# Two transformer blocks on one core: later modulation columns, finer norm pieces with unread products at the joints, bias sums on VectorE

## The reference

```python
def first_block(x, c, ...):
    mod = (silu(c) @ w_ada + b_ada)              # 6 x 1024: shift, scale, gate for mixer and FFN
    h = rms_norm(x, g_pre_mix) * (1 + sc_m) + sh_m
    y = hybrid_mixer(h, ...)                     # NSA group + DSA group, then w_out
    x = x + ga_m * rms_norm(y, g_post_mix)
    h = rms_norm(x, g_pre_ffn) * (1 + sc_f) + sh_f
    return x + ga_f * rms_norm(swiglu(h, w_gate_up, w_down), g_post_ffn)

def compress(k, pe, w1, b1, w2, b2):             # inside the NSA group, for keys and for values
    blocks = k[:, idx] + pe                      # 31 overlapping blocks of 32 tokens
    return gelu(flatten(blocks) @ w1 + b1) @ w2 + b2
```

## Time and profile before

| | before |
|---|---|
| median of 3 runs | 2392.31 us |
| the profiled execution | 2389.78 us, of which the span is 2387.7 us |
| mean granted TensorE clock | 0.974 of full |
| TensorE (matmul) busy | 2284.4 us, 96% |
| VectorE / ScalarE / GpSimd busy | 43% / 21% / 29% |
| DMA, mean busy share of 16 engines | 33%, 105 GB/s |

### The profile page before, as it was taken

One profiled execution on the slowest core, in us unless ns is written; L12 is line 12 of the kernel. 1 busy time (PEld: TensorE's weight loads), 2 busy tenths in 40 slices (PEclk: granted clock), 3 DMA queues, 4 the chain that ended last, 5 costly groups with the idle time before them and its releaser, 6 DMA issues. The chain is left out here.

```text
span 2387.7 us, 26637 instructions
## 1 busy us (share of the span) xinstructions
PE 2284.4 (96%) x10499; PEld 1766.8 (74%) x10499; DVE 1022.1 (43%) x1899; ACT 492.3 (21%) x1131; POOL 683.5 (29%) x549
## 2 busy tenths in 40 slices
PE   7999999899999999999999999997999899999998
PEld 3454667667757888888778888884556668888887
DVE  4556854454325752244554223542623422112354
ACT  3101332233344000010300011112133532000002
POOL 0000000000010655564155555520010104555642
PEclk9999889899999999999999999998999999999999
DMA  9533334453421454233335432331122122222230
GB/s 323 178 133 105 108 103 145 159 169 101 120 77 65 141 172 146 66 85 81 106 111 171 141 95 66 81 106 35 36 75 71 36 71 71 71 96 70 73 98 36
DMA packets 255287, 250.14 MB, mean 105 GB/s; under 512 B 19874, under 2 KB 207420, under 8 KB 255036
## 3 DMA queue, kind: packets, MB, share of 16 engines
q1 hardware_dynamic: 254728, 248.30, 33.0%
q10 hardware_dynamic: 436, 0.15, 0.0%
HBM read 243.19 MB, written 4.19 MB: 104 GB/s over the span
## 5 line engine op out<-in xcount | busy, mean ns | idle before, releaser
L1975 POOL TENSOR_TENSOR w_sums<-ring 128x512 f32<-128x512 f32 x66 | 90.3, 1368 | 514.0 <-POOLq L1306 330.3
L2001 POOL TENSOR_TENSOR hidden<-rstd,h_act 128x256 f32<-128x256 f32 x66 | 53.8, 816 | 401.4 <-DVE h_act L2177 401.4
L1860 PE MATMUL ps<-h_sums,w_sums 128*128 128x256 f32 x528 | 128.9, 384 | 6.0 <-DVE h_sums L2113 5.6
L814 PE MATMUL ps<-h_act,ring 128*128 128x512 f32 (+1 forms) x288 | 128.3, 599 | 5.2 <-PEq L333 4.4
L2177 DVE TENSOR_TENSOR h_act<-ps,rstd 128x256 f32<-128x256 f32 x78 | 33.0, 424 | 232.3 <-PE ps L1878 136.1
L1878 PE MATMUL ps<-h_sums,ring 128*128 128x256 f32 x528 | 125.8, 381 | 2.5 <-DVE rstd L2156 2.2
L1866 PE MATMUL ps<-h_act,ring 128*128 128x256 f32 x528 | 126.5, 383 | 0.0
L1872 PE MATMUL ps<-h_sums,w_sums 128*128 128x256 f32 x528 | 125.1, 380 | 1.0 <-DVE rstd L2149 1.0
L1826 PE MATMUL ps<-h_act,ring 128*128 128x256 f32 x528 | 125.2, 381 | 0.0
L1883 PE MATMUL ps<-h_act,w_sums 128*128 128x256 f32 x528 | 124.7, 379 | 0.0
L1834 PE MATMUL ps<-h_act,ring 128*128 128x256 f32 x528 | 124.5, 379 | 0.0
(11 more groups left out here) (463 smaller groups left out, 4461.8 us busy)
## 6 DMA issues: line engine op xcount, KB each, us to landing
ring<-in_ffn_w_in SPq DMA_DIRECT2D x66, 1024.0 KB, 7.7
ring<-in_w_ada SPq DMA_DIRECT2D x12, 2048.0 KB, 7.9
ring<-in_w_mod SPq DMA_DIRECT2D x12, 2048.0 KB, 8.0
ring<-in_w_gate_up SPq DMA_DIRECT2D x22, 1024.0 KB, 8.0
ring<-in_ffn_w_out SPq DMA_DIRECT2D x32, 704.0 KB, 6.2
ring<-in_w_in SPq DMA_DIRECT2D x6, 2048.0 KB, 8.1
ring<-in_ffn_w_out SPq DMA_DIRECT2D x8, 1408.0 KB, 7.0
ring<-in_w_down SPq DMA_DIRECT2D x16, 704.0 KB, 5.8
```

Of the source, the lines that this page charges most:

```text
L814: last = pe.matmul(K.ps[i % 3][0:rows, :], lhs(w, item, j, k), hl(k), start=(k == 0), stop=(k == KT - 1))
L1860: last = pe.matmul(pb, s2[:, k], F.t2[:, k], start=(k == 0), stop=(k == 3))
L1975: pool.tensor_tensor(s1, a21, a22, ALU.add).then_inc(S["wsum"].sem, 1)
L2001: pool.tensor_tensor(one[:, j], F.gate1[f % 2], F.got21[f % 2], ALU.mult)
```

## The change

Four parts, in one diff.

1. Selector: the bias sum `pe @ w1` is formed by VectorE, 32 instructions of 128x128, two interleaved sums, before `weigh(1)`; TensorE needs one product for each of the two parts. `prob_scores(0)` and `(1)` come before the latent keys and values, and these take two context products after each, instead of none between and 8 afterwards. The number of context products before `prob_turn(0)` is the same (48).
2. Attention: `modulation_columns` for ada 4+j moves from tile f = 9+2j to f = 10+2j (the last two to down tiles 1 and 3), with two buffers for the sums instead of one.
3. Joints: x is updated and squared in three pieces (4, 2, 2 tiles of 128 features) instead of two, multiplied by the root in three (2, 3, 3); ScalarE scales all of the first half before it takes the second root; TensorE runs 15 products of ones by ones, 128 columns, that nobody reads, after `x_sum(0)` in the joints after out1, the first and second FFN and out2, and 38 at the end of `stage_ffn_1_2`.
4. Second FFN call: GpSimd starts its first weight sums when x is updated (before: when the normed h is written) and its second when VectorE's first eight h sums are done; VectorE starts the modulation sums at odd units in call 1.

```diff
@@ selector @@
+    pesum = K.sem("lc_pesum")
-    free = (2, 5, 3, 4)
...
                     if m % 4 == 3:
                         context(1)
-                for m in range(16):
-                    last = pe.matmul(K.ps[3 + i][:, 64:65], w[:, i, m, :], K.p("cmp_pe", 16 * i + m, 1),
-                                     start=(m == 0), stop=(m == 15))
-                    if m % 4 == 3 and m < 15:
-                        context(1)
-                last.then_inc(hidm, 1)
-                context(1)
+                pe.wait_ge(pesum, 31 + i)
+                pe.matmul(K.ps[3 + i][:, 64:65], M.cstd[:, P * i:P * i + P], K.ones[:, 0:1], start=True,
+                          stop=True).then_inc(hidm, 1)
+                context(4)
...
             pe.wait_ge(rel, 24)
-            for j in range(4):
-                if j == 2:
-                    pe.wait_ge(cmk, 2)
-                pe.matmul(K.ps[free[j]][:, :], M.wuk[:, 2 * j:2 * j + 2, :], M.cT[:, :], start=True, stop=False)
-                pe.matmul(K.ps[free[j]][:, :], const(K, "esel", ROPE), M.kr[:, :], start=False,
-                          stop=True).then_inc(kvm, 1)
-            for t in range(QT):
-                pe.wait_ge(kvk, t + 1)
-                pe.matmul(K.ps[free[t]][:, :], M.cT[:, t * P:t * P + P], M.wuv[:, :, :].rearrange("p h d -> p (h d)"),
-                          start=True, stop=True).then_inc(kvm, 1)
-            context(8)
-            pe.wait_ge(kvk, 4 + QT)
+            pe.wait_ge(cmk, 2)
             prob_scores(0)
             prob_scores(1)
-            context(40)
+            for n in range(4 + QT):
+                if n >= 2:
+                    pe.wait_ge(kvk, n - 1)
+                dst = K.ps[n % 2][:, :]
+                if n < 4:
+                    pe.matmul(dst, M.wuk[:, 2 * n:2 * n + 2, :], M.cT[:, :], start=True, stop=False)
+                    last = pe.matmul(dst, const(K, "esel", ROPE), M.kr[:, :], start=False, stop=True)
+                else:
+                    t = n - 4
+                    last = pe.matmul(dst, M.cT[:, t * P:t * P + P], M.wuv[:, :, :].rearrange("p h d -> p (h d)"),
+                                     start=True, stop=True)
+                last.then_inc(kvm, 1)
+                context(2)
+            context(32)
+            pe.wait_ge(kvk, 4 + QT)
             prob_turn(0)
... (VectorE, after the four norm products and before weigh(1))
+            w = K.ring.take(dve, "cmp").rearrange("p (i m h) -> p i m h", i=2, m=16)
+            for m in range(16):
+                for i in range(2):
+                    part, at = M.cstd[:, P * i:P * i + P], K.p("cmp_pe", 16 * i + m, 1)
+                    if m:
+                        dve.wait_ge(pesum, 2 * m - 1 + i)
+                        ins = dve.scalar_tensor_tensor(part, w[:, i, m, :], at, part, ALU.mult, ALU.add)
+                    else:
+                        ins = dve.tensor_scalar(part, w[:, i, m, :], at, None, ALU.mult)
+                    ins.then_inc(pesum, 1)
@@ attention @@
-    late_sums = lambda m, v: K.rstd[:, 0, :]
+    late_sums = lambda m, v: K.rstd[:, m % 2, :]
...
-            columns = {CTX_SCORER + 2 * j + 1: (("ada", 4 + j), late_sums) for j in range(7)}
+            columns = {CTX_SCORER + 2 * j + 2: (("ada", 4 + j), late_sums) for j in range(6)}
+            more = {1: (("ada", 10), late_sums), 3: (("ada", 11), late_sums)}
...
-                    context_down(K, X, pe, d, (("ada", 11), late_sums) if d == 1 else None) for d in range(KT)))
+                    context_down(K, X, pe, d, more.get(d)) for d in range(KT)))
...
-            steps = itertools.chain.from_iterable(modulation_steps(K, dve, ("ada", 4 + j), late_sums, 1)
+            steps = itertools.chain.from_iterable(modulation_steps(K, dve, ("ada", 4 + j), late_sums, 2)
@@ tails @@
+NEW_PIECES = ((0, 4), (4, 6), (6, KT))
+NORMED_PIECES = ((0, 2), (2, 5), (5, KT))
...
-    for b in range(2):
-        y = T.y(4 * b, 4 * b + 4, HALF * t, HALF * t + HALF)
-        S["turned"].wait(dve, 2 * t + b + 1)
-        dve.tensor_tensor(x_part(K, t, b), x_part(K, t, b), y, ALU.add).then_inc(S["x_new"].sem, 1)
+    for k0, k1 in NEW_PIECES:
+        y = T.y(k0, k1, HALF * t, HALF * t + HALF)
+        S["turned"].wait(dve, 2 * t + (1 if k1 <= 4 else 2))
+        dve.tensor_tensor(x_part(K, t, k0, k1), x_part(K, t, k0, k1), y, ALU.add).then_inc(S["x_new"].sem, 1)
...
+def idle_products(K, pe, bank, n):
+
+    for _ in range(n):
+        pe.matmul(K.ps[bank][:, 0:P], K.ones[:, :], K.ones[:, :], start=True, stop=True)
... (tail_scalar)
     h_scaled(K, T, act, 0, range(0, 4))
+    h_scaled(K, T, act, 0, range(4, KT))
     x_root(K, T, act, 1)
-    h_scaled(K, T, act, 0, range(4, KT))
... (end of out_tensor; the same with bank 2 at the end of fast_tail_tensor)
     x_sum(K, O.T, pe, 0, 1)
+    idle_products(K, pe, 5, 15)
... (stage_ffn_1_2, after the last fast_tail_tensor)
                 x_sum(K, F1.T, pe, 1, 1)
+                idle_products(K, pe, 2, 38)
@@ fast_gpsimd, fast_vector @@
     if call == 1:
-        F.prev.s["normed"].wait(pool, 4)
+        F.prev.s["x_new"].wait(pool, 6)
     up_weight_sums(0)
+    if call == 1:
+        S["hsum"].wait(pool, 8)
     up_weight_sums(1)
...
-            if u // 2 < len(F.late) and u % 2 == 0:
+            if u // 2 < len(F.late) and u % 2 == F.call:
                 steps = modulation_steps(K, dve, ("mod", F.late[u // 2]), late, 2)
```

More of the change, by code:

```diff
@@ L1504, in __init__ @@
         self.s = {n: Tally(K.tail[n], K.tail_base[n]) for n in TAIL_SEMS}
-        counts = dict(squared=len(pieces), scaled=len(pieces), added=len(self.adds), y_sum=2, y_root=2, turned=4, x_new=4)
+        counts = dict(squared=len(pieces), scaled=len(pieces), added=len(self.adds), y_sum=2, y_root=2, turned=4, x_new=6)
         if scale is not None:
-            counts.update(x_sq=4, x_sum=2, x_root=2, normed=4, h=2 * KT)
+            counts.update(x_sq=6, x_sum=2, x_root=2, normed=6, h=2 * KT)
         for n, count in counts.items():
@@ L1578, in x_update @@
         dve.tensor_tensor(y, y, r, ALU.mult).then_inc(S["turned"].sem, 1)
[L1579 to L1582 removed]
+    for k0, k1 in NEW_PIECES:
+        y = T.y(k0, k1, HALF * t, HALF * t + HALF)
+        S["turned"].wait(dve, 2 * t + (1 if k1 <= 4 else 2))
+        dve.tensor_tensor(x_part(K, t, k0, k1), x_part(K, t, k0, k1), y, ALU.add).then_inc(S["x_new"].sem, 1)
 def x_square(K, T, act, t):
[L1587 to L1589 removed]
+    for i, (k0, k1) in enumerate(NEW_PIECES):
+        T.s["x_new"].wait(act, 3 * t + i + 1)
+        act.activation(T.squares[t][:, k0:k1, :], x_part(K, t, k0, k1), ACT.Square).then_inc(T.s["x_sq"].sem, 1)
 def x_sum(K, T, pe, t, b):
[L1594 to L1596 removed]
+    for i in ((0,), (1, 2))[b]:
+        T.s["x_sq"].wait(pe, 3 * t + i + 1)
+        for k in range(*NEW_PIECES[i]):
+            last = pe.matmul(K.ps[6 + t][:, 0:HALF], K.ones[:, :], T.squares[t][:, k, :], start=(k == 0),
+                             stop=(k == KT - 1))
     if b:
@@ L1609, in x_normed @@
 def x_normed(K, T, dve, t):
-    r = K.tmp[:, 1, HALF * t:HALF * t + HALF].unsqueeze(1).broadcast_to([P, 4, HALF])
     T.s["x_root"].wait(dve, t + 1)
-    for b in range(2):
-        dve.tensor_tensor(h_part(K, t, b), x_part(K, t, b), r, ALU.mult).then_inc(T.s["normed"].sem, 1)
+    for k0, k1 in NORMED_PIECES:
+        r = K.tmp[:, 1, HALF * t:HALF * t + HALF].unsqueeze(1).broadcast_to([P, k1 - k0, HALF])
+        dve.tensor_tensor(h_part(K, t, k0, k1), x_part(K, t, k0, k1), r, ALU.mult).then_inc(T.s["normed"].sem, 1)
 def h_scaled(K, T, act, t, ks):
     for k in ks:
-        T.s["normed"].wait(act, 2 * t + k // 4 + 1)
+        T.s["normed"].wait(act, 3 * t + sum(k >= a for a, _ in NORMED_PIECES))
         h = K.h[:, k, CTX + HALF * t:CTX + HALF * t + HALF]
@@ L2802, in turn @@
                     T = F.T.s["x_new"]
-                    T.wait(pe, 2 * (t // 2) + half + 1)
+                    T.wait(pe, 3 * (t // 2) + (3 if half else 1))
                     if i >= 4:
```

17 lines of the change are left out of this document (6 added, 11 removed).

## The result

The changed kernel has a median of 2374.29 us (four runs, 2372.78 to 2378.64); the kernel before, run beside it, 2393.95. The ratio is 0.9924, with a 95% interval of 0.9903 to 0.9945. The profiled execution took 2372.78 us, its span 2371.0, at a mean clock of 0.981 (before: 2389.78, 2387.7, 0.974).

A forecast was written before the change was run, and what follows sets the result against it. TensorE was taken to bound the kernel, busy nearly all the time. Selector -12, attention +10 and joints -15 sum to -17, so the median goes from 2392.3 to 2375 us, range 2360 to 2388.

The forecast's parts named there:

- Selector, -12: Selector: removing one-column products gives 6.6 us and returning clock 5.4; -12 us, bounds -15 and -6.
- Attention, +10: Attention: waits for sums become waits for context loads, with columns and low clock on the path; +10 us, bounds 0 and +13.
- the columns' 6.5 us: Attention: columns in tile 10+2j lie on the repeating path, 0.9 to 1.02 us each, about +6.5 us.
- Joint after out1, -1.9: Joint after out1: unread products fill the pause and keep the clock up for the second `x_sum`; -1.9 us.
- After out2, -2.7: Joint after out2: unread products fill the pause and keep the clock up for the second `x_sum`; -2.7 us.
- First to second FFN, -7 and -1.1: Between the FFNs: GpSimd gates, clock and wait give -7 us (bounds -8.5 and -4.5); later modulation units give -1.1.
- Joint to mixer 2, -2.5: After the second FFN: earlier block end -1.8 us (bounds -3 and +1), plus 0.7 if the clock is up at mixer 2.
- (1): Attention rival: the column waits go and no load takes their place; 2354 us, chance 12%.
- (2): Selector rival: only -5 us, since ScalarE's order keeps TensorE or the low level stays; 2382 us, chance 15%.
- (3): Joints rival: unread products don't hold the clock, only the second FFN's start gains, -7 us; 2383 us, chance 13%.
- (4): Joints rival: the unread products themselves run at the low level, together +19 us; 2410 us, chance 5%.
- -5 the right sum for a full block: First to second FFN joint: if three `x_normed` pieces each wait for one GpSimd instruction, 3.9 us, -5 instead of -7.

The follow-up runs named there:

- the experiment: The changed kernel without any of the unread products (15 in four joints, 38 at the end of the second FFN): 2382.24 us, ratio 0.9963 to the kernel before.
- sums two pairs early: The changed kernel with each modulation sum of attention begun two pairs earlier on VectorE (the first two can't be): 2338.20 us.
- after: The changed kernel itself, all four parts in, against the kernel before: median 2374.29 us, ratio 0.9924.
- columns back: The changed kernel with its attention part undone (modulation columns in their old tile, one buffer for the sums): 2364.85 us, ratio 0.989 to the kernel before.
- first sum early: The changed kernel, sums two pairs earlier, first sum partly before the first pair, with 30 unread products at the second FFN's end or none there: 2331.27 and 2331.96 us.

## Why the prediction was right, point by point

The forecast was 2375, measured 2374.3. The direction and the mechanism of each part held, but that the total fits this well is luck: attention lost 5.8 us more than forecast, and the stretch of the two FFNs gained 3.4 more, the joint to mixer 2 0.9 more and the unchanged start 1.1.

- **Selector, -12: right (-12.7), but its split was wrong.** I put 6.6 us on the products and 5.4 on the clock, part of this for the new order. The bias sum on VectorE gave 13.4 us in either order (125.9 - 112.5 with the old one, 126.6 - 113.2 with the new one), the order nothing that can be seen. In the trace, from the first `compress` product to L630's sixteen records it is 23.9 us instead of 35.9, and these records 1.8 less: 6.6 for the products, 1.3 for the shorter wait behind them, the rest clock. The second window of low clock did not go, it moved. On VectorE two errors cancelled: the idle time before `divide(0)` was 3.9 us and not 1, but five short waits for ScalarE, 4.3 us together, went as well, which I had not counted. The idle time before `centre(0)` went with the old order too, so my reason for it was wrong. The new work took 8.3 us instead of 8.5; the wait for `prob_turn(2)` grew to 4.3, as the text allowed.
- **Attention, +10: right in mechanism, too small.** The part alone costs 9.4 and 11.6 us by medians and 12.8 and 16.7 by traces, against bounds of 0 and 13. The mis-sized terms are the waits (I had them 3.0 us shorter, they are 10.8 us longer between the two kernels with the new selector) and the low clock (7 taken, 1.6 found). How much of the waiting is the columns' 6.5 us can't be separated: from one context load's issue to the next, the six stretches are 0.4 to 4.4 us longer with the columns in tile 10+2j, 11.0 together, and not 0.95 each. The other 3.0 us of the 15.8 aren't undone with the columns: in tile 10 TensorE goes on 9.4 us after the issue of the load instead of 8.2, and the eight records behind take 3.78 us instead of 1.99.
- **Joint after out1, -1.9: -1.7. After out2, -2.7: -2.6.** Both are the unread products by the experiment (1.7 and 2.7). After out2 this is the joint by itself (31.98 us before, 29.36 after); that the whole stretch from mixer 2 on gives 2.6 too is luck, since it varies by more.
- **First to second FFN, -7 and -1.1: -11.5.** The gates gave 7.1 where I had 3.6 + 0.9 - 0.7 = 3.8: I took 2.9 us of the first unit's loss as left, 1.1 are (11.64 against 10.56), and without the gates the first unit is 18.2 us, not 17.1. The odd units gave 3.8 where I had 1.1, from half of one wait's label. The unread products gave 1.1 where I had 3.2: the 6.72 us of the earlier trace rows was not the price of a joint without them, the experiment had 5.19. 7.1 + 3.8 + 1.1 = 12.0 against 11.5 measured; the stretch varies by about 1.3 us among kernels with the same instructions (827.4 to 828.7).
- **Joint to mixer 2, -2.5: -3.4.** From the second `x_sum` to the first gate product it is 15.4 us instead of 17.8, and the gate products take 19.0 instead of 20.0. The first term was mis-sized: without any unread products it is 14.5, so the finer pieces gave 3.3 us, and the 38 products cost 1.0 of them. These ran at full clock in 8.65 us and ended 1.7 us after ScalarE:

```profile
1608.45 8.65 PE L1580 MATMUL ps<-ones 128*128 128x128 f32 x76
...
1611.38 4.04 ACT L1645 ACTIVATE h_act<-h_act,mod,coef 128x256 f32<-128x256 f32 x8 [0.76 <-DVE h_act L1637]
1617.36 1.28 ACT L2398 ACT_TABLE_LOAD   x1 [1.94 <-PEq L2228]
...
1620.31 1.10 PE L2331 MATMUL ps<-ring,x_res 128*128 128x512 f32 x2 [3.21 <-DMA g_bias<-in_f_bias]
...
1621.40 2.06 PE L2331 MATMUL ps<-ring,x_res 128*128 128x512 f32 x2
...
1623.53 1.72 PE L2331 MATMUL ps<-ring,x_res 128*128 128x512 f32 x2
```

  ScalarE's scaling ends at 1615.4, the block at 1617.1 with the products; the next one begins with one group of gate products at the full level (1.10 us), one at the low (2.06) and one that is partly at the low (1.72). With 30 products the way to the first gate product is 13.9 us, as with none at the end (13.8), so then they no longer hold the end.
- **Rivals.** (1), the waits gone with nothing in their place, gave 2354: refuted by the waits of L621. (2), selector -5, (3), unread products that don't hold the clock, and (4), at the low level: refuted by 12.7, 3.72 and 8.65 us.

On the sharing of SBUF, VectorE's three `x_normed` pieces beside GpSimd's early sums, the three together, then the second and the third by themselves, and the three pieces of the other half of the tokens, with GpSimd idle:

```profile
1179.91 4.58 DVE L1637 TENSOR_TENSOR h_act<-x_res,tmp 128x512 f32<-128x512 f32 x3
```

```profile
1180.51 2.03 DVE L1637 TENSOR_TENSOR h_act<-x_res,tmp 128x768 f32<-128x768 f32 x1
```

```profile
1182.46 2.02 DVE L1637 TENSOR_TENSOR h_act<-x_res,tmp 128x768 f32<-128x768 f32 x1
```

```profile
1186.94 2.43 DVE L1637 TENSOR_TENSOR h_act<-x_res,tmp 128x512 f32<-128x512 f32 x3 [2.46 <-ACT tmp L1629]
```

```profile
1180.07 1.65 POOL L2000 TENSOR_TENSOR w_sums<-ring 128x512 f32<-128x512 f32 x1 [37.54 <-DVE x_res L1603]
...
1181.80 1.87 POOL L2002 TENSOR_TENSOR w_sums<-w_sums,ring 128x512 f32<-128x512 f32 x1
...
1183.63 1.99 POOL L2003 TENSOR_TENSOR ring<-ring 128x512 f32<-128x512 f32 x1
...
1185.58 1.27 POOL L2005 TENSOR_TENSOR w_sums<-ring,w_sums 128x512 f32<-128x512 f32 x1
```

The three pieces take 4.58 us instead of 2.43, and GpSimd's instructions 1.65 to 1.99 instead of 1.27. So the early start costs 2.15 us on VectorE, not the 3.9 that I worked out from a full block; of these 0.2 reach TensorE (`product_1` begins 3.8 us after the second `x_sum`, and 3.6 with GpSimd's old gates). Nor was -5 the right sum for a full block: 3.9 in place of 0.7 makes -3.8. The ends of the instructions tell how they share. VectorE's second and third piece end at 1182.54 and 1184.48, each 0.8 us after a GpSimd instruction has ended (1181.72 and 1183.67); GpSimd's second and third end 1.1 us after these pieces. That is a little less than what a piece and a GpSimd instruction take alone, 0.95 and 1.27 us. So from the second piece on the two engines took turns, an instruction at a time, and each waited only for the rest of the other's instruction, about 1.1 us per piece; the first piece, begun before GpSimd, wasn't held up. The Trainium skill (SBUF — State Buffer, Who interferes with whom) says that such a pair contends and calls the shared pair of ports an exclusive lock. The rows agree: taking turns is what such a lock gives. What was wrong was the count of three pieces that each wait for a whole instruction.

## What to carry to other kernels

A wait names what came last, not what would come next: before taking it away, look which load its releaser starts, and in which instant. Here VectorE's sum, not TensorE's columns, held the ring; moving the columns cost 9 to 12 us and moving the sums gained 32 to 43. Narrow products can cost more than their own time: here 32 one-column products of 6.6 us cost 13.4, with the wait and the low clock behind them.

## What the runs showed of the hardware that was not expected

- Unchanged code took another time from kernel to kernel. The selector, from its first scores, took 112.4 to 113.3 us in seven kernels with the bias sum on VectorE (one of them with the old order), 115.5 in three and 118.2 in one, otherwise with the same instructions. Most of the difference is how long the low level lasts after `prob_scores`; with the sums two pairs early:

```profile
290.00:300.00 10.00, 10.00 (x16) 4.64 (x16) 8.97 (x18) 1.20 (x2) 0.00 (x0) 0.50 0.00 0
```

  0.50 where after has 0.99. The start of the selector varied too, from 231.5 to 234.4 us, and so did the stretch from mixer 2's gate products to the last FFN's last down products: 712.7 to 717.5 us in the eleven kernels with unread products. There the 4.6 us between after and columns back lie in a few groups of matmul records of mixer 2 and out2 that ran at the low level in one trace and not in the other. What decides this was not found; an edit of a few microseconds has to be read from its own stretch.
- The first context load of attention took 9.3 to 9.7 us from issue to landing in the nine kernels in which attention began at 344 to 350 us and waited for it, and 8.1 to 8.2 in the three in which it began near 359. In the two kernels with the first sum early attention also began at 345 to 348, but the load was issued 8 to 10 us behind its beginning instead of 12 to 15, and took 8.1. So when attention begins is not by itself what decides. Whether other traffic is the reason stays open; it wasn't tried.
- 128-column products of ones ran at 0.23 us each without a break, and with 15 of them in a pause of 3.9 us the second `x_sum` behind it ran at the full level throughout in all 44 joints (3.72 us); without them in none of 12 (5.19 to 6.78).
